# Squares of the tokens by dimension, and the gates' chain beside the dense steps, in a hybrid mixer block on one core

## What is computed

```python
def rmsnorm(x, w, eps=NORM_EPS):
    y = xf * lax.rsqrt(jnp.mean(xf * xf, axis=-1, keepdims=True) + eps)
    return y * w
...
n = rmsnorm(x, attn_norm[l])
u = n @ w_in[l]                       # gates, GDN, mLSTM, RG-LRU, RWKV columns
g = -jnp.exp(a_log) * jax.nn.softplus(a_raw + dt_bias)     # from the gates' columns
...
mem_n = rms_norm(mem, norm_mem_g)     # 256 memory tokens
mkv = mem_n @ w_mem_kv
```

## Time and profile before

| | |
|---|---|
| median of 3 runs | 2432.63 us (2432.6 to 2434.78) |
| profiled execution | 2434.96 us, span 2433.2 us |
| busy: TensorE / VectorE / ScalarE / POOL | 98% / 59% / 46% / 5% of the span |
| mean granted TensorE clock | 0.993 |
| DMA, first 41.4 us | 309 GB/s; over the span 183 GB/s |

### The profile page before, as it was taken

One profiled execution on the slowest core, in us unless ns is written; L12 is line 12 of the kernel. 1 busy time (PEld: TensorE's weight loads), 2 busy tenths in 40 slices (PEclk: granted clock), 3 DMA queues, 4 the chain that ended last, 5 costly groups with the idle time before them and its releaser, 6 DMA issues.

```text
span 2433.2 us, 32292 instructions
## 1 busy us (share of the span) xinstructions
PE 2395.0 (98%) x13430; PEld 1991.1 (82%) x13430; DVE 1433.0 (59%) x1855; ACT 1129.4 (46%) x1424; POOL 117.5 (5%) x83
## 2 busy tenths in 40 slices
PE   8899999999999999999999999999999999999998
PEld 7687888878888888888888888888888888888887
DVE  4866658577755555555555575555446655555555
ACT  6645435554554444444434464445444455344444
POOL 0110111220000000000000040000000000000000
PEclk9999999999999999999999999999999999999999
DMA  9543344645555555555555566555545545555564
GB/s 327 192 140 122 122 140 162 215 160 182 198 188 178 189 190 190 190 190 190 182 191 185 186 204 231 188 173 174 173 156 189 169 144 171 193 190 184 194 242 141
DMA packets 245618, 445.65 MB, mean 183 GB/s; under 512 B 7393, under 2 KB 72545, under 8 KB 242657
## 3 DMA queue, kind: packets, MB, share of 16 engines
q1 hardware_dynamic: 241984, 423.65, 52.9%
q0 software_dynamic: 2912, 19.40, 2.1%
q10 hardware_dynamic: 576, 0.53, 0.1%
HBM read 433.07 MB, written 10.49 MB: 182 GB/s over the span
## 4 chain that ended last, share of the span: by engine, by line
PE 90%; DVE 6%; ACT 2%; issue 1%; DMA 1%; SPq 0%; ACTq 0%; DVEq 0%
PE pp L644 24%; PE pp L646 24%; PE pp L645 24%; PE pp L673 7%; PE pp L674 3%; DVE ringL L1956 2%; PE ps L603 2%; DVE AR L2461 1%; DMA raw<-in_w_in 1%; PE ps L1250 1%; PE ps L1264 1%; PE ps L777 1%; ACT ringH L1338 1%; PE ps L830 0%; DVE AR L1964 0%
## 5 line engine op out<-in xcount | busy, mean ns | idle before, releaser
L1338 ACT CAST ringH<-raw 128x1024 fp32r<-128x1024 f32 x779 | 814.8, 1050 | 1002.2 <-PE pp L646 870.4
L1956 DVE TENSOR_TENSOR ringL<-raw,ringH 128x1024 fp32r<-128x1024 f32 x779 | 952.3, 1242 | 462.3 <-ACT ringH L1338 461.4
L644 PE MATMUL pp<-ringH,nS 128*128 128x512 f32 x1376 | 545.1, 396 | 3.9 <-DVE ringL L1956 2.8
L646 PE MATMUL pp<-ringH,nS 128*128 128x512 f32 x1376 | 536.5, 390 | 0.0
L645 PE MATMUL pp<-ringL,nS 128*128 128x512 f32 x1376 | 536.0, 390 | 0.0
L673 PE MATMUL pp<-nS,ringH 128*128 128x512 f32 x992 | 367.4, 411 | 10.4 <-DVE ringL L1956 5.4
L644 PEld LDWEIGHTS pp<-ringH,nS 128*128 128x128 f32 x1376 | 258.4, 188 | 59.7 <-DVE ringL L1956 6.1
L646 PEld LDWEIGHTS pp<-ringH,nS 128*128 128x128 f32 x1376 | 258.2, 188 | 54.6
L645 PEld LDWEIGHTS pp<-ringL,nS 128*128 128x128 f32 x1376 | 258.6, 188 | 51.1 <-issue 0.2
L674 PE MATMUL pp<-nS,ringL 128*128 128x256 f32 x992 | 280.5, 283 | 0.0
L644 PE MATMUL pp<-ringH,xS 128*128 128x512 f32 x704 | 277.2, 394 | 0.0
(11 more groups left out here) (392 smaller groups left out, 1957.7 us busy)
## 6 DMA issues: line engine op xcount, KB each, us to landing
raw<-in_w_in SPq DMA_DIRECT2D x189, 1024.0 KB, 5.1
raw<-in_ffn_w_gate SPq DMA_DIRECT2D x44, 1024.0 KB, 5.2
raw<-in_ffn_w_up SPq DMA_DIRECT2D x44, 1024.0 KB, 5.2
raw<-in_ffn_w_down SPq DMA_DIRECT2D x44, 1024.0 KB, 5.1
raw<-in_w_out SPq DMA_DIRECT2D x32, 1024.0 KB, 5.2
raw<-in_w_mem_kv SPq DMA_DIRECT2D x16, 1024.0 KB, 5.3
raw<-in_w_proj_a SPq DMA_DIRECT2D x8, 1024.0 KB, 5.1
raw<-in_w_proj_m SPq DMA_DIRECT2D x8, 1024.0 KB, 5.2
```

What stands on the lines that cost most here:

```text
L644: mm(o, XH[:, ts(j)], WH, first, False)
L646: t_of[0] = mm(o, XL[:, ts(j)], WH, False, last)
L1338: e.copy(ringH[:, h % NSPL, 0:nh * cols], raw[:, u % NRAW, h0 * cols:(h0 + nh) * cols]).then_inc(*hi.tick(h))
L1956: tt2(ringL[:, h % NSPL, o], raw[:, u % NRAW, h0 * cols:(h0 + nh) * cols], ringH[:, h % NSPL, o].bitcast(F32), SUB).then_inc(*lo.tick(h))
```

## The change

The row tokens of x and of the memory are no longer loaded. The squares are taken of `x_dim` and `mem_dim` on ScalarE into `sqs` (`squares_of`), VectorE adds 16 tiles to one (`fold`, 2048, 1024, 512 and 256 columns wide), and a product with ones sums over the partitions (`total`): columns 0 to 255 hold each token's sum in all partitions, two more hold it by row. From it come the mean squares (`mean_square`), roots of both (`root`) and reciprocals of both, 256 and 2 columns wide (`one_over`). The stage `gates` keeps only the product; all that follows is a new stage `scan`, which runs together with `mem`, from step 36 on. The zeroing of `gateS` is done first in `norm`. SyncE sends `w_gates` ahead of the masks, and `params` one unit of weights earlier.

```diff
 def beside_rwkv(L):
-    yield from L.stage("mem")
+    scan = L.stage("scan")
+    for _ in range(2):
+        next(scan)
+        yield
+    for _ in L.stage("mem"):
+        next(scan, None)
+        yield
+    yield from scan
...
-        memk = v3(GU, 2, D)
+        sqs = v3(GU, 16, T)
...
-            def factor(key, mk_p, mk_v, r):
-
-                e.wait_ge(*mk_v.at("r"))
+            def total(key, mk_p, mk_v):
+
+                e.wait_ge(*mk_v.at("sum"))
                 b = take(key, "r")
+                m1(b[:, 0:T], ones, sqs[:, 0, :], True)
                 for tt in range(2):
-                    t = m1(b[:, ts(tt)], r[:, tt:tt + 1].broadcast_to([128, 128]), ident, tt == 0)
+                    t = m1(b[:, T + tt:T + tt + 1], sqs[:, 0, ts(tt)], ones[:, 0:1], False)
...
+            def squares_of(ma, src, ks):
+                act(sqs[:, ks, :], src[:, ks, :], ACT.Square).then_inc(*ma.tick("sq", ks.stop))
...
+            def scan(L):
+                for h in range(2):
+                    squares_of(nx_a, x_dim, slice(8 * h, 8 * h + 8))
+                    yield
...
+            def fold(mv, *widths):
+
+                for n in widths:
+                    own(mv)
+                    tt2(sqs[:, 0:n, :], sqs[:, 0:n, :], sqs[:, n:2 * n, :], ADD).then_inc(*mv.tick(*(("sum",) if n == 1 else ())))
+
+            def mean_square(key, mp, mv, r, rows):
+
+                e.wait_ge(*mp.at("r"))
+                tsc(rows, ring.of(key, "r")[:, 0:T], 1.0 / D, 1e-6, MUL, ADD).then_inc(*mv.tick())
+                tsc(r, ring.of(key, "r")[:, T:T + 2], 1.0 / D, 1e-6, MUL, ADD).then_inc(*mv.tick("ms"))
+                ring.free(mv.now(), key, "r")
+
+            def one_over(ma, mv, r, rows):
+
                 e.wait_ge(*ma.at("rt"))
                 e.reciprocal(r, r).then_inc(*mv.tick("r"))
...
+                e.reciprocal(rows, rows).then_inc(*mv.tick("rb"))
...
-                for tt in range(2):
-                    e.dma_start(xtok[:, tt, :], I["x"][0, ts(tt), :]).then_inc(s_xt[tt], 16)
...
-                for tt in range(2):
-                    e.dma_start(memk[:, tt, :], I["mem_2"][0, ts(tt), :]).then_inc(s_m[tt], 16)
```

More of the change, by code:

```diff
@@ L734, in gates @@
                 yield 3
-                yield 3
+            def scan(L):
+                for _ in range(3):
+                    yield
+                e.wait_ge(s_i, 16)
+                total("nx", nx_p, nx_v)
+                for _ in range(7):
+                    yield
                 zr, bs, gc, e_, m_ = grows
@@ L748, in gates @@
                 t.then_inc(*gt_p.tick("col"))
-                yield
+                for _ in range(3):
+                    yield
             def mem(L):
[L752 to L758, removed]
+                for _ in range(11):
+                    yield
+                total("me", me_p, me_v)
+                for _ in range(4):
+                    yield
             def bcast(mk, name, o):
@@ L1448, in unit, with to_hi @@
                     place_rope(blocks[s.block.n - 1].tag)
-            def to_hi(key, src, landed, ma, gain, put, held, square, turns):
+            def to_hi(key, src, landed, ma, gain, put, held, squared):
                 for n in range(8):
@@ L1461, in to_hi, with root @@
                             sent[0] = 1
-                    if n in turns:
-                        square(turns.index(n))
+                    if n in squared:
+                        squares_of(ma, src, slice(4 * n - 16, 4 * n - 12))
                     yield
[L1466 to L1475, removed]
+            def squares_of(ma, src, ks):
+                act(sqs[:, ks, :], src[:, ks, :], ACT.Square).then_inc(*ma.tick("sq", ks.stop))
+            def root(mv, ma, r, rows):
                 e.wait_ge(*mv.at("ms"))
+                act(rows, rows, ACT.Sqrt).then_inc(*ma.tick())
                 act(r, r, ACT.Sqrt).then_inc(*ma.tick("rt"))
@@ L1485, in norm @@
                 act(small[:, 126:127], small[:, 127:128], ACT.Copy).then_inc(*nx_a.tick())
+                e.copy(gateS[:, 0:2048], small[:, 127:128].broadcast_to([128, 2048])).then_inc(*gt_a.tick("z"))
                 e.wait_ge(s_an, 16)
[L1487 to L1498, removed]
+                yield from to_hi("nx", x_dim, {c.start: s for c, s in zip(x_parts, s_x)}, nx_a, lambda k: pc("attn_norm", k), lambda k: nS[:, k, 0, :], lambda n: None, ())
                 gH = gateS[:, 0:2048].rearrange("p (k g c) -> p k g c", k=16, g=4)[:, :, :, 0:4]
@@ L1503, in gates, with scan @@
                 yield
+            def scan(L):
+                for h in range(2):
+                    squares_of(nx_a, x_dim, slice(8 * h, 8 * h + 8))
+                    yield
+                yield
+                yield
+                root(nx_v, nx_a, rx, rxb)
+                yield
                 zr, bs, gc, e_, m_ = grows
@@ L1515, in gates @@
                 act(gc, gc, ACT.Ln, bias=csg[:, 2:3]).then_inc(*gt_a.tick("ln"))
-                yield
-                yield
-                yield
+                for _ in range(6):
+                    yield
                 e.wait_ge(*gt_v.at("mm"))
@@ L1919, in scalar @@
             course(lane(unit, {
-                "norm": norm, "gates": gates, "mem": mem, "rwkv": rwkv, "mlstm": mlstm,
+                "norm": norm, "scan": scan, "mem": mem, "rwkv": rwkv, "mlstm": mlstm,
                 "gdn": gdn, "rglru": rglru,
@@ L2105, in gates, with scan @@
                 yield
+            def scan(L):
+                yield
+                e.wait_ge(*nx_a.at("sq", 16))
+                fold(nx_v, 8)
+                yield
+                fold(nx_v, 4, 2, 1)
+                yield
+                yield
+                mean_square("nx", nx_p, nx_v, rx, rxb)
+                yield
+                one_over(nx_a, nx_v, rx, rxb)
+                own(nx_v)
                 zr, bs, gc, e_, m_ = grows
-                e.wait_ge(s_h, 16)
-                e.wait_ge(s_c, 48)
                 e.wait_ge(*gt_p.at("g"))
@@ L2184, in mem @@
                     pass
+                e.wait_ge(*me_a.at("sq", 16))
+                fold(me_v, 8)
                 yield
-                yield from factor("me", me_p, me_a, me_v, 116, rmb)
+                fold(me_v, 4, 2, 1)
+                yield
+                yield
+                yield
+                mean_square("me", me_p, me_v, rm, rmb)
+                yield
+                yield
+                one_over(me_a, me_v, rm, rmb)
                 yield
```

65 lines of the change are left out of this document (27 added, 38 removed).

## The result

| | before | changed kernel |
|---|---|---|
| median | 2433.33 us (2432.6 to 2434.78, 5 runs) | 2444.29 us (2441.91 to 2447.51, 5 runs) |
| ratio of the medians | | 1.0047, 95% interval 1.0035 to 1.0058 |
| profiled span | 2433.2 us | 2445.1 us |
| mean granted TensorE clock | 0.993 | 0.991 |

The change costs 11.0 us by the medians, 11.9 by the two spans. The forecast was 2442.0, slower, in a range of 2433 to 2449. The decisive step was named rightly, but terms of the sum were wrong in opposite senses, and one claim beside it was false. The profiled execution of the changed kernel, at 2446.86 us, is its second longest of five; the two longest have a mean granted clock of 0.991, the other three (2441.91 to 2444.29 us) 0.993.

What follows compares the result with a forecast made beforehand. VectorE was taken to bound 75.97 to 111.43 us, TensorE the rest. A start 6.5 us later plus a longer stretch gave +10.1, less 0.6: +9.5 us, 2442 for the median, range 2433 to 2449.

Steps and rivals of the forecast that it cites:

- The sum's wait at 52: At step 48, TensorE waits 2 us for VectorE's sum of the squares of x; step 64 starts at 67.7.
- Row factors: Behind the sum on VectorE: factors for all tokens ready at 66.0 us, with 1.85 us for the 256-column reciprocal.
- The POOL queue: First memory-tile store queues behind three products needing row factors, lands at 75.4; step 68 at 79.2, RWKV rows at 82.5 (+6.5).
- VectorE's stretch: From the RWKV rows on, VectorE is the bound: 39.1 us instead of 35.5, ending at 121.6 against 111.43 (+10.1).
- Of this 0.6 comes back: At the stretch's end: 0.6 us regained because the memory's product now stands ahead of that point.
- Their 4 MB buy nothing: Early in the kernel: dropping the row-token loads gains nothing, since no TensorE wait there is for them.
- The dips of TensorE's clock: Low clock behind each long wait falls in time TensorE waits again; none counted but the last, present before too.
- The hidden store: Rival: memory-tile store lands before ScalarE asks, RWKV rows near 71.4; -1.5 us, 2431; chance 0.15.
- TensorE as the bound of the stretch: Rival: VectorE's added work fits idle time, TensorE needs only its 30.3 us; 11 us sooner, 2422; chance 0.07.
- The memory table: Rival: its 2 MB load lands after ScalarE wants it at 48.0, or stores are slower; 2445 to 2450; chance 0.12.
- high bound: Slower products, later store landing, late reciprocal and late memory table together: about +15.5 us, top of 2437 to 2448.
- late reciprocal: Term of the high bound: the second long reciprocal, costed at nothing in the sum, adds 0.5, to 1.4 us.

Runs made afterwards that it cites:

- e7: e3 with TensorE's product for the sum of the squares of x one piece (four steps) later: 2436.71 us, ratio 1.0010.
- e1: Changed kernel with POOL's products of w0 to w2 put off to w3's place, behind the first two stores of the memory tiles: 2438.33 us, ratio 1.0022.
- e6: e3 without the memory's adds of 2048, 1024 and 512 columns on VectorE, so its sums lack most terms: 2430.82 us, ratio 0.9989.
- e2: Changed kernel with the memory's sum read from PSUM by VectorE right behind its small reciprocal in the first half of RWKV: 2441.18 us, ratio 1.0032.
- e3: Changed kernel with the edits of e1 and e2 together: 2435.55 us, ratio 1.0009.
- e4: Kernel before without its four row-token loads (4 MB), squares taken of the tables by dimension, row factors wrong: 2430.22 us, ratio 0.9982.
- e11: e3 with the squares' adds on TensorE, x's row factors and VectorE's add and multiply of zr each one piece earlier: 2428.99 us, ratio 0.9981.
- e12: e11 with GpSimd's products of w0, w1 and w2 made to wait for VectorE's zr: 2428.34 us, ratio 0.9975.

## Why the prediction was right or wrong

**The sum's wait at 52: right.** 2.2 us for 2.0, step 64 at 67.53 for 67.7. That it costs nothing in the end I hadn't said; e7 shows it.

**Row factors: right.** 64.95 for 66.0. The 256-column reciprocal took 1.73 us, where I took 1.85 by the line through the small ones; the plain bound of 0.42 was far off. My estimate from the Trainium skill ("VectorE: DVE Perf Modes", walkthrough of the 8-slice pipeline), 2.2, was farther off than the line.

**The POOL queue: right, and the decisive step.** The products took 4.47 us for 4.6, the first store landed 4.2 us after its issue for 4.8, step 68 at 77.47 for 79.2, RWKV rows at 80.60 for 82.5. e1 shows the cause by removing it: 6.0 us of the 11.0. The first store's landing agrees better with the estimate from the Trainium skill ("DMA: Bandwidth & Descriptors", anatomy of one DMA on the gpsimd path), 4.4, than with the median I took; all four took 4.1 to 7.7 us, with a median of 5.1.

**VectorE's stretch: the bound right, the size somewhat high.** It took 37.7 us for 39.1; e6 confirms that work of VectorE counts there. The memory's adds took 5.7 us for 4.6, because the first, beside a product of POOL, took 3.28. With start and length off by 1.9 and 1.4 us the end came 7.1 us later, not 10.1 (the forecast counted to TensorE's product at 111.43, 0.2 us behind VectorE's read).

**"Of this 0.6 comes back": failed twice.** I treated the memory's product as moved work, and asked neither what wait it would fill nor who would need its PSUM slot. The long wait at that point is gone (in before 3.7 us, and its products at the low clock; in the changed kernel the same products take 2.2 us instead of 4.0), so that step 102 was only 5.5 us late. And the slot then held back L609 for 3.16 us, with the low clock behind it: 3.1 us from step 102 to 110 and 1.8 more to step 140. e2 shows that cause, 3.1 us by the medians, and e3 against e1 2.8. My sum of +9.5 lies near the measured 11.0 by luck: the end of the stretch was forecast 3.0 us too late, and the delay that follows it was forecast at -0.6 where the profiled spans have +4.8 (3.3 of it up to step 140). Another slot wait, 2.1 us at L912 for the gates' instructions behind the 3.28 us add, was missed as well.

**"Their 4 MB buy nothing, for no wait of TensorE here is for them": false.** e4: 3.5 us. I read TensorE's list of waits only one engine deep. ScalarE's rows at 28.03 and 31.41, idle for a DMA, were in the trace of before.

**"The dips of TensorE's clock ... fall in time in which it waits again, so I count none but the last": half right.** It holds up to the stretch (e7), not for the new wait at 130, behind which TensorE alone sets the pace.

**The rivals.** The hidden store is refuted by ScalarE's 6.9 us wait, and TensorE as the bound of the stretch by VectorE's 94% there. The memory table was not late: it landed 11.1 us after its issue, and ScalarE rounds its first tile at 47.47 us without a wait for it. A slip in the high bound: its terms add up to +15.1 with 0.5 for the late reciprocal and to +16.0 with 1.4, where I wrote +15.5. Nothing rests on it.

The last 1.5 us, between step 140 and the end of the profiled spans, are the clock's, in work that is the same in both kernels. Steps 200 to 300, then 300 to 400, first before, then now:

```profile
248.96:362.98 114.02, 112.12 (x1327) 95.28 (x1326) 67.24 (x130) 43.80 (x59) 12.61 (x6) 1.00 0.43 134
362.98:430.87 67.89, 66.02 (x468) 58.31 (x467) 50.95 (x68) 38.93 (x59) 12.13 (x7) 0.98 0.53 176
259.42:376.37 116.95, 115.05 (x1327) 97.76 (x1326) 67.21 (x130) 43.80 (x59) 12.62 (x6) 0.97 0.41 130
376.37:442.85 66.48, 64.68 (x469) 56.90 (x467) 50.95 (x68) 38.23 (x59) 12.11 (x7) 1.00 0.52 171
```

The granted clock is 0.97 in one stretch and 1.00 in the other, where the kernel before has 1.00 and 0.98: 2.9 us more and 1.4 less. Whether the change brings this about stays open, since only one execution of it was profiled; by the medians the whole loss is 11.0, not 11.9.

## What to carry to other kernels

When a buffer's store shares a queue with other work, ask what that work waits for; one reordering on an engine that is busy for 5% of the span cost 6 us. For each product that is moved, follow its PSUM slot up to the read that frees it, and for each wait follow the releaser back until it is a DMA or an engine that never idles. Where VectorE is the bound and TensorE's sum in PSUM is cheap, let TensorE do the adding.

## What the runs showed of the hardware

A VectorE instruction of 128 x 4 elements lasted 3.96 us instead of 0.17 while three products of GpSimd ran back to back (e11), and 0.17 again once they were moved (e12). In e12 another one of 128 x 4 elements (L2199, at 66.21 us) lasted 1.16 us instead of 0.15, until the last of the three products ended. The same three products took 3.49 us with VectorE held and 4.47 to 4.79 us where VectorE had low halves or memory tiles, which took 2.06 us (for 1.22) and 2.74 to 2.76 us (a pair, for 0.87) there. The Trainium skill ("SBUF — State Buffer", Who interferes with whom) says that the two engines share a port pair as an exclusive lock, so that the second to issue fully blocks until the first finishes, where VectorE's instruction is in a 2-port mode or has two inputs in SBUF and GpSimd's reads SBUF. The traces agree with blocking. They don't show its order so: in e11 the small instruction stands as begun at 61.84, 0.43 us ahead of the first product, and it was not let in between the products.

A product of ones in fp32r over 16 slices of 256 columns took 2.08 us on TensorE, for which VectorE's adds took 4.7 us alone and 5.7 beside GpSimd.

The reciprocal of 256 columns takes 1.73 us on both of its uses, 6.8 ns a column against 1.6 for the plain instruction of that width (0.42 us).
